# Two heads of both key groups in one attention unit, products alternating between the array's row halves

## What is computed

```python
def sink_attention(q, k, v, dist, valid, sinks):
    qg = q.reshape(b_, c_, lq, KV_HEADS, Q_PER_KV, HEAD_DIM)     # 2 key groups, 4 heads each, 64
    s = jnp.einsum('bcqkgd,bcskd->bckgqs', qg, k).astype(jnp.float32) * (HEAD_DIM ** -0.5)
    s = s - slopes * dist.astype(jnp.float32)[None, :, None, None]
    s = jnp.where(valid[None, :, None, None], s, jnp.finfo(jnp.float32).min)
    ...
    p = jax.nn.softmax(jnp.concatenate([s, sink], axis=-1), axis=-1)[..., :-1]
    out = jnp.einsum('bckgqs,bcskd->bcqkgd', p.astype(v.dtype), v)
```

## Time and profile before

| | |
|---|---|
| median of 3 runs | 1561.44 us (1558.61 to 1562.68) |
| profiled execution | 1555.33 us, span 1553.7 us |
| TensorE busy | 1463.9 us (94% of the span), 6,907 products |
| VectorE busy | 1228.6 us (79%) |
| ScalarE busy | 1040.6 us (67%) |
| GpSimd busy | 183.2 us (12%) |

### The profile page before, as it was taken

One profiled execution on the slowest core, in us unless ns is written; L12 is line 12 of the kernel. 1 busy time (PEld: TensorE's weight loads), 2 busy tenths in 40 slices (PEclk: granted clock), 3 DMA queues, 4 the chain that ended last, 5 costly groups with the idle time before them and its releaser, 6 DMA issues.

```text
span 1553.7 us, 21012 instructions
## 1 busy us (share of the span) xinstructions
PE 1463.9 (94%) x6907; PEld 1212.4 (78%) x6907; DVE 1228.6 (79%) x1024; ACT 1040.6 (67%) x980; POOL 183.2 (12%) x237
## 2 busy tenths in 40 slices
PE   5999599289999999999999999999999999999898
PEld 5887487168888888888888888888888888888676
DVE  4144734759888889999888888999988888898775
ACT  4365522257777777777777777777777777777645
POOL 6000000511011111110111101111011111010000
PEclk9999799589999999999999999999999999999999
DMA  9012055369999999999999999999999999998631
GB/s 320 23 63 82 1 217 195 96 254 387 374 376 376 366 370 378 362 375 368 374 370 375 373 365 371 369 373 373 369 370 380 369 370 381 360 386 287 228 125 42
DMA packets 109065, 465.90 MB, mean 300 GB/s; under 512 B 19058, under 2 KB 24698, under 8 KB 76266
## 3 DMA queue, kind: packets, MB, share of 16 engines
q1 hardware_dynamic: 93978, 445.24, 75.6%
q0 software_dynamic: 14432, 18.94, 3.5%
q10 hardware_dynamic: 624, 1.31, 0.3%
HBM read 457.50 MB, written 24.96 MB: 311 GB/s over the span
## 4 chain that ended last, share of the span: by engine, by line
PE 76%; DVE 2%; ACT 1%; DMA 1%; issue 0%; DVEq 0%; POOL 0%; SPq 0%; ACTq 0%; POOLq 0%
PE bank L2081 30%; PE bank L2084 15%; PE bank L2102 15%; PE bank L2107 7%; PE bank L78 4%; PE bank L2073 2%; PE bank L2052 2%; PE bank L2063 2%; DMA w_slot<-in_w_dn 1%; DVE wg_lo L2008 0%; DVE h_in L1968 0%; PE bank L2165 0%; ACT wg_hi L1825 0%; DMA xg<-hn_rows,idx_in 0%; ACT pair_hi L1680 0%
## 5 line engine op out<-in xcount | busy, mean ns | idle before, releaser
L1862 DVE TENSOR_TENSOR pair_lo<-w_slot,pair_hi 128x2048 fp32r<-128x2048 f32 x384 | 870.5, 2288 | 114.5 <-ACT pair_hi L1680 114.5
L1680 ACT ACTIVATE pair_hi<-w_slot 128x2048 fp32r<-128x2048 f32 x384 | 737.0, 1921 | 262.6 <-PE bank L2084 175.2
L2081 PE MATMUL bank<-pair_hi,xg_hi 128*128 128x512 f32 x1024 | 274.6, 390 | 0.8 <-issue 0.8
L2084 PE MATMUL bank<-pair_lo,xg_hi 128*128 128x512 f32 x1024 | 273.9, 389 | 0.0
L2081 PE MATMUL bank<-pair_hi,xg_lo 128*128 128x512 f32 x1024 | 273.9, 389 | 0.0
L2081 PEld LDWEIGHTS bank<-pair_hi,xg_hi 128*128 128x128 f32 x1024 | 192.7, 188 | 41.7 <-issue 1.5
L2081 PEld LDWEIGHTS bank<-pair_hi,xg_lo 128*128 128x128 f32 x1024 | 192.5, 188 | 40.1
L2084 PEld LDWEIGHTS bank<-pair_lo,xg_hi 128*128 128x128 f32 x1024 | 192.2, 188 | 39.9
L2102 PE MATMUL bank<-pair_hi,aT_hi 128*128 128x512 f32 x496 | 135.7, 395 | 0.0
L2107 PE MATMUL bank<-pair_lo,aT_hi 128*128 128x512 f32 x496 | 133.0, 390 | 0.0
L2102 PE MATMUL bank<-pair_hi,aT_lo 128*128 128x512 f32 x496 | 132.9, 390 | 0.0
(11 more groups left out here) (301 smaller groups left out, 1426.5 us busy)
## 6 DMA issues: line engine op xcount, KB each, us to landing
w_slot<-in_w_gu SPq DMA_DIRECT2D x256, 1024.0 KB, 7.0
w_slot<-in_w_dn SPq DMA_DIRECT2D x128, 1024.0 KB, 7.1
raw<-in_w_in SPq DMA_DIRECT2D x3, 2048.0 KB, 22.6
y_in<-expert_rows SPq DMA_DIRECT2D x3, 2048.0 KB, 10.2
raw<-in_w_o SPq DMA_DIRECT2D x2, 2048.0 KB, 9.3
raw<-in_w_ple_gate SPq DMA_DIRECT2D x2, 2048.0 KB, 11.0
uq<-in_x_prompt SPq DMA_DIRECT2D x4, 512.0 KB, 8.3
h_rows<-uq SPq DMA_DIRECT2D x4, 512.0 KB
```

The source lines that it names most:

```text
L1680: nc.scalar.activation(pair_hi[pair(b, k)][:], w_slot[k + down][:], ACT.Copy).then_inc(hi_ready, 1)
L1862: mine(nc.vector.tensor_tensor(pair_lo[pair(b, k)][:], w_slot[k + down][:], pair_hi[pair(b, k)][:].bitcast(F32), ALU.subtract), lo_ready)
L2081: nc.tensor.matmul(bank[:, n, :], x[:, c, :], w_hi[:, n * CB:(n + 1) * CB], start=False, stop=False)
L2084: last = nc.tensor.matmul(bank[:, n, :], xg_hi[:, c, :], w_lo[:, n * CB:(n + 1) * CB], start=False, stop=c == KC - 1)
```

## The change

A unit is now a block n and a pair p of heads of each key group: heads 2p and 2p + 1 of group 0 and the same of group 1. There are eight units as before. TensorE's four score products alternate between the groups, so between partitions 0 to 63 with bank 4 and 64 to 127 with bank 5. `alibi` is laid out in the order of the units (`head_place`). VectorE's operations take the sinks and write the outputs with one more level in their access patterns, since a unit's heads are no longer neighbours in them. The value products take the columns of the head's own group.

```diff
-    UNITS = [(n, g) for n in range(NT) for g in range(KV)]
+    HP = HG // KV
+    UNITS = [(n, p) for n in range(NT) for p in range(HG // HP)]
...
+    def head_place(h):
+
+        g, i = divmod(h, HG)
+        return i // HP * HG + g * HP + i % HP
+
     def score_banks(u):
-        return bank[:, 4:6, :].rearrange("p b (i s) -> p (b i) s", s=2 * P)
+        return bank[:, 4:6, :].rearrange("p g (i s) -> p g i s", s=2 * P)
...
-                mine(nc.gpsimd.tensor_scalar(alibi[:, h, :], dist_f[:], -SLOPES[h], None, ALU.mult))
+                mine(nc.gpsimd.tensor_scalar(alibi[:, head_place(h), :], dist_f[:], -SLOPES[h], None, ALU.mult))
...
-                mine(nc.vector.scalar_tensor_tensor(pr[:, :, lo:2 * P], score_banks(u)[:, :, lo:2 * P], HD ** -0.5,
-                     alibi[:, g * HG:(g + 1) * HG, lo:2 * P], ALU.mult, ALU.add), score_read)
+                mine(nc.vector.scalar_tensor_tensor(pr[:].rearrange("p (g i) s -> p g i s", g=KV)[:, :, :, lo:2 * P],
+                     score_banks(u)[:, :, :, lo:2 * P], HD ** -0.5,
+                     alibi[:, p * HG:(p + 1) * HG, lo:2 * P].rearrange("p (g i) s -> p g i s", g=KV),
+                     ALU.mult, ALU.add), score_read)
...
-                sk = sink_b[:, g * HG:(g + 1) * HG]
-                mine(nc.vector.tensor_tensor(st[:, 0, :], st[:, 0, :], sk, ALU.max))
+                sk = sink_b[:].rearrange("p (g i) -> p g i", g=KV)[:, :, p * HP:(p + 1) * HP]
+                by_group = [st[:, x, :].rearrange("p (g i) -> p g i", g=KV) for x in range(3)]
+                mine(nc.vector.tensor_tensor(by_group[0], by_group[0], sk, ALU.max))
...
-                mine(nc.vector.tensor_tensor(st[:, 2, :], sk, st[:, 1, :], ALU.add), max_ready)
+                mine(nc.vector.tensor_tensor(by_group[2], sk, by_group[1], ALU.add), max_ready)
...
-                    uq[:, n, CB + g * HG * HD:CB + (g + 1) * HG * HD].rearrange("p (i d) -> p i d", i=HG),
-                    o_bank(u), st[:, 5, :].unsqueeze(2).to_broadcast([P, HG, HD]), ALU.mult), pv_read)
+                    uq[:, n, CB:2 * CB].rearrange("p (g i d) -> p g i d", g=KV, i=HG)[:, :, p * HP:(p + 1) * HP, :],
+                    o_bank(u).rearrange("p (g i) d -> p g i d", g=KV),
+                    st[:, 5, :].rearrange("p (g i) -> p g i", g=KV).unsqueeze(3).to_broadcast([P, KV, HP, HD]),
+                    ALU.mult), pv_read)
...
-                for i in range(HG):
-                    last = nc.tensor.matmul(score_banks(u)[:, i, lo:2 * P], qT[g * HD:(g + 1) * HD, n, i, :],
-                                            kT[g * HD:(g + 1) * HD, (n - 1) * P + lo:(n + 1) * P],
-                                            start=True, stop=True)
+                for i in range(HP):
+                    for kv in range(KV):
+                        last = nc.tensor.matmul(score_banks(u)[:, kv, i, lo:2 * P],
+                                                qT[kv * HD:(kv + 1) * HD, n, p * HP + i, :],
+                                                kT[kv * HD:(kv + 1) * HD, (n - 1) * P + lo:(n + 1) * P],
+                                                start=True, stop=True)
...
-                                                v_nat[:, n - 1 + j, g * HD:(g + 1) * HD],
+                                                v_nat[:, n - 1 + j, i // HP * HD:(i // HP + 1) * HD],
```

More of the change, by code:

```diff
@@ L547, in exps @@
             def exps(u):
-                n, g = UNITS[u]
+                n, p = UNITS[u]
                 lo = P if n == 0 else 0
```

## The result

The changed kernel takes 1553.9 us (median of 10 runs, 1551.28 to 1559.66), the kernel before 1560.51 us (10 runs, 1556.28 to 1562.68). The ratio is 0.9965, with a 95% interval from 0.9949 to 0.9982: faster by 0.35%, 5.5 us. (The two medians lie 6.6 us apart, 0.42%, the two lowest runs 5.0 us; the runs of either kernel spread over 6 to 8 us, so each of these is loose by a microsecond or more.) The profiled execution took 1552.84 us, its span is 1551.2 us.

What follows compares the result with a forecast made beforehand. TensorE's time plus the places where it stands was taken as the bound. Of 6.1 us array time saved, 5.4 us reaches the join; off the median 1561.44 us this gives 1556.0 us, range 1552.0 to 1563.0.

Steps and rivals of the forecast that it cites:

- the 5.4 us of the stage: Attention stage: how much earlier its end was forecast, out of 6.1 us of array time saved; whole-saving case, chance 0.57.
- Nothing added or removed: Whole change: same units, products, transposes and exps, no added wait or moved DMA; VectorE's longer access patterns cost nothing.
- A pair at the time of one: Score products: two row halves run in one product's time, saving 0.45 us in units 0 and 1, 0.86 in others.
- Rivals 1 and 4: Score products: 1, long streams don't overlap, gain 0 to 0.9 us (0.17); 4, alternation exposes weight loads, 1567.7 us (0.07).
- Staggered pairs: Score products: program order makes four products need five steps instead of eight; gain 4.1 us, 1557.3 us; chance 0.10.
- What reaches the join: Join of all engines ending the attention stage: 5.4 us arrives; most of unit 7's saving doesn't, as VectorE comes late.
- the long gap: TensorE's 3.06 us wait before 125.06 for a split weight: stays as long, comes 3.48 us earlier.
- the last values: Last unit's value products at 165.89 us: start 5.4 us earlier, the gap before them growing from 1.11 to about 1.8.
- The clock: Attention stage's two 1.2 GHz stretches: taken as unchanged, no cost; another of 3.4 us would cost 1.7 us.
- rival 3: Whole saving but one more low clock stretch, behind the longer gap or elsewhere: gain 3.7 us, 1557.7 us; chance 0.09.
- The offset: Whole kernel: the median of three runs lies 6.1 us above the profiled execution's 1555.33 us; carried over to the forecast.

Runs made afterwards that it cites:

- e2_grouped: Changed kernel with each unit's four score products ordered group 0, 0, 1, 1 instead of alternating; 1557.79 us, ratio 0.9977 to the kernel before.
- e11_sample_four: Kernel before with the sample score products in runs of four of one group instead of alternating; 1560.83 us in one profiled run.
- e12: Kernel before with the new kind of unit in the last block only (units 6 and 7); 1557.61 us in one profiled run.
- e13: Kernel before with the new kind of unit in blocks 1 and 2 only (units 2 to 5); 1556.58 us in one profiled run.
- e10_sample_far: Kernel before with the sample score products in runs of eight of one group instead of alternating; 1560.69 us in one profiled run.
- e5_fill_expert: Changed kernel plus 24 unneeded identity products on TensorE ahead of the transposes of the first expert's tokens; 1556.76 us, ratio 0.9970 to the kernel before.
- e8_fill_gaps: Changed kernel plus unneeded identity products in two attention-stage waits: 10 behind the sample scores, 5 ahead of the last values; 1552.33 us, ratio 0.9949.
- e14_before_fills: Kernel before plus three identity-product fills: behind the sample scores, ahead of the last values, ahead of the router's transposes; 1555.29 us, ratio 0.9968.
- e9_fill_gaps_router: Changed kernel plus three identity-product fills: two in the attention stage, one ahead of the router's first transposes; 1549.28 us, ratio 0.9938 to the kernel before.

## Why the prediction was right

The forecast was 1556.0 us, 0.35% less than before. Measured: 1553.9 us, and 0.35% less by the ratio of the runs. The mechanism and the 5.4 us of the stage are shown by the traces. That the end shows the same share to the hundredth of a per cent is in part luck: the medians alone would say 0.42%, the ratio's interval reaches from 0.18% to 0.51%, and the one pair of profiles says 2.5 us.

- *Nothing added or removed.* Held: the same counts; VectorE's read at L713 takes 1.22 to 1.23 us as at L706, so the longer access patterns cost nothing that shows.
- *A pair at the time of one.* Held for the long streams too, for which the kernel before had no row: 0.215 us a pair (1.13 us = 0.48 + 3 x 0.215), and 4 steps less a unit. Rivals 1 and 4 fall by this; the price of changing halves is zero to within 0.01 us a record.
- *Staggered pairs* (rival 2, from the page's rule that products start in program order) fall: the pair begins together in the profile after, and e2_grouped and e11_sample_four show records started past others. Where the Trainium skill's "TensorE: Matmul & The Clock Gate", Part 3, says strict order, these runs differ for products in different row halves; its statement that such products run at once is what the trace shows.
- *What reaches the join.* 3.48 us at the long gap (measured 3.64 - 0.16), 5.4 us at the last values (5.58 - 0.16), the gap there 1.69 us against 1.8. The split by units was tested by e12 and e13 and holds.
- *The clock.* The term was left at zero, with one more low stretch as rival 3. In the stage itself one less came, and it was worth about 0.4 us at the join (27.48 us from the last values against 27.12 in e10_sample_far), not the 1.7 us that I priced a stretch of 3.4 us at. Behind the join, where I had written that every transfer and product starts relative to it, the pair of profiles gave back 3.7 us to low stretches that stood elsewhere. That sentence is the weak one of the working: true of the order of the work, not of its times. But the profiles of the other kernels show that what was given back belongs to the single executions, above all to a quick one of the kernel before, and not to the change. Over the runs it about averaged out; the single pair shows 2.5 us, less than half of the gain.
- *The offset.* I set the profiled run 6.1 us below the median and carried that over. It was a run with a high mean clock (0.969), not a cost of the profile or its absence; the changed kernel's profiled run lies 1.1 us below its median. The forecast in the end was the median less 5.4 us, so it wasn't touched by this. It was 2.1 us too high: 0.9 us because the median of the kernel before is 1560.51 over ten runs and not 1561.44 as over three, 1.2 us because the medians lie 6.6 us apart. The changed kernel met high mean clocks more often (10 of its 22 runs had 0.966 and more, against 13 of the 64 runs of the kernel before beside the experiments; but 3 of 12 in e2_grouped, whose trace is the same).

What stays open: whether and why the changed kernel meets the low stretches less often. The one behind the last values stands in three of the four profiles without fills in the stage where unit 7 is an old one (not in e10), and in one of the seven where it is new (e5); that is too few to build on. The fills show that TensorE's waits in this stage have a part in it; the place of a low stretch in a single run could not be steered.

## What to carry to other kernels

Small fp32 products with 64 rows cost half when two that lie in different row halves and write different banks stand within four records of each other, as far as these runs reach; look for units that hold only one half, and give them both. Cost such a gain at the point where the next engine takes over: the last unit's share is lost if that engine comes late anyway. And before reading a gain of a few microseconds out of two profiles, lay the granted clock beside them stage by stage, and look whether a further execution shows them in the same places. Filling a wait of some microseconds with products that nobody waits for can keep the clock up and cost nothing; it did so in e8_fill_gaps and e14_before_fills, half of the way in e9_fill_gaps_router, and not in e5_fill_expert, where the fill ended 4.84 us too early.

## What the runs showed of the hardware

- Products in different row halves are started past waiting ones of the other half, up to four records behind (e2_grouped; in e11_sample_four pairs start with the fifth record, in e10_sample_far with the thirteenth).
- Two streams of 256 columns from different halves into different banks run without slowing each other: 0.215 us for the pair, as for one.
- With the clock at 1.2 GHz four products of 512 columns take 2.05 us, at 2.4 GHz 1.07 us. Around the wait behind the sample scores the clock was low for 6.8 us in every profile without the fill. In e10_sample_far it fell at 122.4, while TensorE still ran the sample scores, so the wait alone is not what lowers it. 20 records of identity products in the wait, 2.5 us of work, kept it high in e8_fill_gaps and e14_before_fills; in e9_fill_gaps_router, with the same fill, a stretch of 3.4 us was left, which began under the fill.
